# Value products of the cache attention one step later, row maximum behind the second key transpose

## The reference, cut to what matters

```python
def _online_update(carry, sc, ck):
    m, l, acc = carry
    m_new = jnp.maximum(m, sc.max(-1))
    corr = jnp.exp(m - m_new)
    p = jnp.exp(sc - m_new[..., None])
    acc = acc * corr[..., None] + jnp.einsum('bhtk,bkr->bhtr', p, ck.astype(jnp.float32))
    return (m_new, l * corr + p.sum(-1), acc)

def page_step(carry, pages):
    ck = cache_ckv[layer, pages]
    kp = cache_kpe[layer, pages]
    return _online_update(carry, _latent_scores(q_lat, q_pe, ck, kp), ck), None
```

## Time and profile before

| what | value |
|---|---|
| median of 3 runs | 972.66 us |
| lowest and highest | 965.53 and 984.15 us |
| the profiled execution | 984.15 us |
| its span on the core | 982.1 us |
| mean granted TensorE clock in it | 0.932 |
| PE busy | 880.4 us (90%) |
| DVE busy | 448.3 us (46%) |
| ACT and POOL busy | 266.9 and 120.0 us |

### The profile page before, as it was taken

How to read it: one execution, slowest core, us unless ns; L and a number is a source line. 1 busy time by engine, 2 the same in 40 slices (tenths; PEclk the granted TensorE clock), 3 DMA queues, 4 the chain that set the end, 5 groups by cost and what they waited for, 6 DMA issues and landing times.

```text
span 982.1 us, 20045 instructions
## 1 busy us (share of the span) xinstructions
PE 880.4 (90%) x8856; PEld 795.1 (81%) x8856; DVE 448.3 (46%) x614; ACT 266.9 (27%) x420; POOL 120.0 (12%) x151
## 2 busy tenths in 40 slices
PE   3999887888787999477799979999999999999996
PEld 2998876777676776355568969999999999999996
DVE  5355475675723343599803355343333344222222
ACT  5333211211122333421214343222222322222222
POOL 7002134334200000454000000000000000000000
PEclk9999899999987999579758989999999999999999
DMA  9423558677611000500122221222332222322202
GB/s 277 149 70 99 199 217 306 225 267 280 249 45 43 1 1 1 154 1 0 44 93 86 87 86 43 85 85 87 107 105 85 85 85 85 107 87 75 87 30 87
DMA packets 71571, 105.78 MB, mean 108 GB/s; under 512 B 7500, under 2 KB 63220, under 8 KB 67284
## 3 DMA queue, kind: packets, MB, share of 16 engines
q1 hardware_dynamic: 63940, 62.74, 20.2%
q0 software_dynamic: 7568, 42.11, 11.7%
HBM read 100.85 MB, written 4.00 MB: 107 GB/s over the span
## 4 chain that ended last, share of the span: by engine, by line
PE 78%; DVE 11%; issue 4%; ACT 2%; DMA 2%; POOL 1%; SPq 0%; DVEq 0%; POOLq 0%; ACTq 0%
PE pair L707 9%; PE pair L709 9%; PE pair L708 9%; PE pair L692 7%; PE pair L694 7%; PE pair L693 7%; PE pair L877 4%; PE pair L901 3%; DVE QD L1910 2%; PE pair L993 2%; PE pair L971 2%; PE pair L970 2%; PE pair L725 2%; DVE KT L1684 1%; PE pair L726 1%
## 5 line engine op out<-in xcount | busy, mean ns | idle before, releaser
L707 PE MATMUL pair<-xhi,whi 128*128 128x260 f32 x736 | 209.7, 285 | 4.6 <-DVE xlo L1591 4.6
L708 PE MATMUL pair<-xlo,whi 128*128 128x260 f32 x736 | 208.8, 284 | 0.0
L709 PE MATMUL pair<-xhi,wlo 128*128 128x260 f32 x736 | 208.6, 283 | 0.0
L707 PEld LDWEIGHTS pair<-xhi,whi 128*128 128x128 f32 x736 | 139.8, 190 | 5.0 <-issue 5.0
L708 PEld LDWEIGHTS pair<-xlo,whi 128*128 128x128 f32 x736 | 140.0, 190 | 0.0
L709 PEld LDWEIGHTS pair<-xhi,wlo 128*128 128x128 f32 x736 | 139.7, 190 | 0.0
L694 PE MATMUL pair<-hhi,wlo 128*128 128x260 f32 x352 | 99.4, 282 | 0.0
L692 PE MATMUL pair<-hhi,whi 128*128 128x260 f32 x352 | 99.3, 282 | 0.0
L693 PE MATMUL pair<-hlo,whi 128*128 128x260 f32 x352 | 99.2, 282 | 0.0
L1684 DVE STREAM_TRANSPOSE KT<-KC 128x2048 uint32<-128x2048 uint32 x32 | 73.7, 2304 | 2.6 <-DMA KP<-in_cache_kpe,icur 2.5
L692 PEld LDWEIGHTS pair<-hhi,whi 128*128 128x128 f32 x352 | 66.3, 188 | 0.0
(11 more groups left out here) (329 smaller groups left out, 1781.7 us busy)
## 6 DMA issues: line engine op xcount, KB each, us to landing
wraw<-in_w_gate SPq DMA_DIRECT2D x11, 1024.0 KB, 5.4
wraw<-in_w_up SPq DMA_DIRECT2D x11, 1024.0 KB, 5.4
wraw<-in_w_down SPq DMA_DIRECT2D x8, 1024.0 KB, 5.0
X<-in_x_prompt SPq DMA_DIRECT2D x8, 512.0 KB, 5.4
wraw<-in_w_in SPq DMA_DIRECT2D x4, 1024.0 KB, 5.9
wsame<-in_w_in SPq DMA_DIRECT2D x4, 1024.0 KB, 6.0
wraw<-in_w_out SPq DMA_DIRECT2D x4, 1024.0 KB, 6.6
wraw<-in_w_down SPq DMA_DIRECT2D x4, 768.0 KB, 4.3
```

The source lines that it names most:

```text
L707: mm(out, h[:, k, c], xhi[:, k, tok], start=k == 0, stop=False)
L708: mm(out, h[:, k, c], xlo[:, k, tok], start=False, stop=False)
L709: ins = mm(out, l[:, k, c], xhi[:, k, tok], start=False, stop=k == KD - 1)
```

## The change

In PE's stream the value products of step n-1 stand behind the second half of the scores of step n, where those of step n stood behind its spread. The fourth dense piece of an odd step now stands ahead of the spread. The products of the last step stand behind two `keys_up`. In DVE's stream `cache_probs(n - 1)` comes between the two transposes, and `cache_max(n)` behind the second. ACT's stream follows through `before_spread`. GpSimd's and SP's streams are as they were.

```diff
 def before_spread(n):
 
-    return 16 + 3 * n + n // 2 + 3 if n < STEPS else PIECES
+    return 16 + 4 * n + 4 - (n + 2) // 2 if n < STEPS else PIECES
...
                 dense_piece(k)
                 dense_piece(k + 1)
                 cache_scores(n, 1)
-                dense_piece(k + 2)
+                if n:
+                    cache_values(n - 1)
+                for k in range(k + 2, before_spread(n)):
+                    dense_piece(k)
                 cache_spread(n)
-                k += 3
-                if n % 2 == 1:
-                    dense_piece(k)
-                    k += 1
-                cache_values(n)
+                k = before_spread(n)
             assert k == PIECES
...
             keys_up(0)
             keys_up(1)
+            cache_values(STEPS - 1)
             keys_up(2)
             keys_up(3)
...
                 if n == 11:
                     hi(10)
-            evacuate(dense_done(PIECES - 1))
             hi(11)
...
                 cache_keys(2 * n + 1)
-                cache_max(n)
+                if n:
+                    cache_probs(n - 1)
                 if n + 1 < STEPS:
                     cache_keys(2 * n + 2)
-                cache_probs(n)
+                cache_max(n)
...
+            cache_probs(STEPS - 1)
             lo(11)
```

## The result

The changed kernel takes 1048.72 us (median of 4, 1042.84 to 1054.87); the kernel before, beside it, takes 976.89. The ratio is 1.0823, with a 95% interval of 1.0697 to 1.0949. The forecast was 1038 us, with a range of 1010 to 1062. The profiled executions are 984.15 and 1049.89 us, 66 us apart.

The account below looks back on a forecast made before the run. PE, busy nine tenths, bounded the kernel; the move closes a loop over the five-buffer ring, 13.97 us a step. That ends the stage 45 us later; with 20 for the clock, 65 on 972.66 gives 1038 us, range 1010 to 1062.

Parts of the forecast that it names:

- The ring: Five buffers for cache rows: the gather of half 2n+5 waits for step n's value products, closing a loop of 13.97 us.
- The size of the loop: Cache stage, each step: products, GpSimd, KP landing, transposes and scores sum to 13.97 us, plus 1.43 for the low clock.
- Rival C: Loop in the cache stage: clock low throughout, scores and products both slow, 2.83 us longer, 1058 us; chance 15 in 100.
- Rival B: Loop in the cache stage: it is closed but the clock stays at 2.4 GHz, 1018 us; chance 24 in 100.
- The end of the stage: Cache stage: last dense piece ends 45 us later by the loops, with 20 for the clock 65 us together.
- The even half has slack: Cache stage: the even half's transpose, maximum, exponential and spread have 5 us of slack before the scores that need them.
- The steps on ACT cost nothing: ACT in the cache stage: later exponential and cache_out waits are over before the maximum; without the loop 0.4 us each.
- DVE's wait: DVE's transpose of each odd half from 5 on waits for KP's DMA, 14 times some 5 us.
- (1): DVE: probabilities of step n-1 ahead of half 2n+2's transpose, maximum behind; with (2) at most 10.0 down to 8.4 a step.
- (2): PE: value products of step n-1 behind step n's second scores; both gaps of PE, 1.2 to 1.8 us a step, would close.
- rival A: Cache stage: gaps close, the ring doesn't bind, PE bounds at 8.4 us a step; 29 us saved, 944 us; 3 in 100.
- The sum against the median: Whole kernel: 65 us on the profiled 984.15 would give 1049; against the median of 972.66 the forecast is 1038 us.

Follow-up runs that it names:

- e9: The changed kernel with six ring buffers in place of five and v not kept, run a second time: 979.38 us, 0.998 of the kernel before.
- e1: The kernel before with four ring buffers in place of five, all orders as before: 1028.03 us, 1.059 of the kernel before.
- e10: The changed kernel with index copies and KP gathers of a pair of halves ahead of GpSimd's wait for the value products: 1014.51 us, 1.044 of before.
- e8: The changed kernel with DVE's order of before, so PE's and ACT's new order alone, run a second time: 1044.62 us, 1.075 of the kernel before.
- e5: The kernel before with DVE's new order alone, PE's and ACT's order and the ring of five as before: 1054.23 us, 1.028 of the kernel before.
- r1: The changed kernel itself run again, nothing altered: 1048.69 us, 1.076 of the kernel before by medians.
- e7: The changed kernel with 18 matmuls into unused columns ahead of the second scores of steps 2 to 15: 1022.03 us, 1.049 of the kernel before.
- e11: The kernel before with dense pieces moved behind both halves of the scores, and KP gathered ahead of the products' wait: 965.42 us, 0.994 of before.

## Why the prediction was right, point by point

**The ring is the path that becomes the bound: shown.** More buffers remove the loss (e9), fewer make it in the old order (e1), a shorter path through the gather makes it smaller (e10), and PE's order alone makes the whole of it (e8). The new order on DVE isn't needed for the loss (e8), and PE's new order costs nothing once there are buffers enough (e9). The DMA engines are filled less than before (0.48 from 150 to 300 us, for 0.72 in rows 2), so it isn't transfer time in general. That DVE's order alone would cost nothing isn't shown: e5 was slower, by a loop of its own.

**The size of the loop.** The 14 odd transposes start at 135.02 to 335.06: 13 turns of 15.39 us. The forecast was 13.97 and 1.43, 15.40. That agreement is in part luck: errors of up to 0.5 us cancel, and two more traces with the same loop, r1 and e8, have turns of 15.74 and 15.76. By terms, means over the 13 turns (with 0.16 for the handovers they make the 15.39):

| term | predicted | measured |
|---|---|---|
| products | 1.93, and 1.43 for the clock | 2.88 |
| GpSimd's start to DVE's transpose | 7.59 | 7.34 |
| transposes | 2.90 | 2.90 |
| scores, first matmul to the products | 1.40 | 2.11 |

I put the clock's price on the products alone. In fact the scores ran at half clock in most turns, being the first in the loop after the gap (2.09 us in the turn above), and the products often came back part of the way (2.11 to 3.64). Against e7, which has 1.91 and 1.14 at full clock, the clock costs 1.94 a turn in place of 1.43: 0.97 on each. Three things hid the 0.51. The scores at full clock are 1.14 in the loop and not 1.40: the products start 1.14 behind the first score matmul, and the 1.40 were read up to DVE's start. The products at full clock are 1.91. And GpSimd's path was 0.25 shorter, since KP's landing came to 5.4 on average for the 5.8 that I took. The prediction had named that as a way to be wrong, but it doesn't hold from trace to trace: in r1 and e8 that path is 7.6 us, as predicted. The 3.36 us that I took for products at half clock were not the whole of it either: the slowest took 3.64. Rival C had both pieces at half clock in every turn. For the scores that is nearly what came, for the products it isn't. Rival B, which had the clock at full, needed the filler of e7 to come true.

The Trainium skill's page "TensorE: Matmul & The Clock Gate", section "HAM oscillation", tells of tiles that each start at the lower clock behind a wait for a DMA. The trace agrees, with the 2.09 us of the scores for 1.14. The Trainium skill's page "DMA: Bandwidth & Descriptors", section "Anatomy of one DMA", has a fit that, taken over KC and KP together, gives an estimate of 5.0 us. From the issue of KC at 207.67 to the landing of KP at 214.05 there are 6.4, so the measurement decides against the estimate here.

**The end of the stage.** The last dense piece ended at 345.32, predicted 344.8; before it was 279.84, so 65.5 us against the sum of 65. In r1 the maxima are 4.6 us further apart, so agreement to half a us is luck as well.

**The even half has slack: right.** DVE waited a little for 8 of them, but PE had only one wait a step for keys, at the odd half. (By the prediction's own terms DVE is through with the odd half at 10.6 us, not 10.8; nothing hangs on it.) **The steps on ACT cost nothing: right**, with one thing wrong beside it: I wrote that PE's wait for spread would be gone. It is still there in 12 steps, up to 1.14 us (8.8 in all, 10.2 in 16 before), since the exponential follows a maximum that came later. It lies outside the loop.

**DVE's wait mis-sized.** I wrote "14 times some 5 us". That is PE's gap, 2.4 to 6.3 us, 4.6 on average. DVE had done all it could before, and waited 6.3 to 10.2. The steps, too, are spread wider than the 14 to 16 us that I wrote, from 13 to 18.

**The gain of (1) and (2): almost nothing, even free of the ring.** e9 gives 0.998, where rival A priced the closed gaps at 29 us for 14 steps. In e9 the maxima are 4.1 us closer than before, no more than two traces of one kernel differ. With six buffers DVE still waits for KP in 18 places: the changed order asks for the even transpose ahead of the maximum, so a late gather now holds up the exponential as well. That reading is argued from the waits; no run separates it.

**The sum against the median.** The forecast is 11 us low against 1048.72, and none of that is the stage: the shift of 65 from profile to profile came out as 66. I made the sum against an execution of 984.15 us and then took 11.5 off for the median. One thing that differs between such executions is told in the last section, at its first point: 16 us in one far stage, which the two profiled executions happened to share. How many of the untraced executions of either kernel had them isn't shown, so the 11 us stay open.

## What to carry to other kernels

A ring's buffer is freed by its last reader, so moving that reader one step later costs a step of prefetch, though no transfer is touched. Before such a move, add up the path from that reader through issue, landing and the next consumer back to it, and compare it with the step; if it is longer, the buffers must grow with the move, or what needn't wait (here KP) be taken out of the wait. If a closed loop has a gap in it, and the trace shows a low clock behind such gaps, price the first work after the gap at that clock, and judge experiments on one stage by a row of that stage, since the total has noise from elsewhere.

## What the runs showed of the hardware

**A stage far behind the change has two levels.** The time behind the last maximum is 689 to 693 us in six of the fourteen traces of the table and 705 to 710 in the other eight, with nothing between. The same 32 matmuls tell them apart in every trace. Here in after, then in e8, each with a window:

```profile
L1127 PE MATMUL pair<-qe,Sst x32: 418/498/579, 552.9 to 580.6; 64*128 64x128 f32 x32
...
550.00:580.00 30.00, 28.31 (x97) 19.79 (x96) 1.82 (x6) 2.94 (x6) 0.00 (x0) 0.50 0.27 96
```

```profile
L1127 PE MATMUL pair<-qe,Sst x32: 272/322/373, 563.4 to 579.8; 64*128 64x128 f32 x32
...
563.00:580.00 17.00, 15.87 (x90) 11.37 (x88) 1.82 (x6) 2.56 (x5) 0.00 (x0) 1.00 0.37 134
```

Their median is 498 ns in one and 322 in the other. Shortly ahead of these matmuls the granted clock was at 0.50 in both. In e8 it was back at 1.00 as they began; in after it stayed at 0.50 throughout, though PE was busy for 28.31 of 30 us. Both profiled executions of the comparison, before and after, have the 498. The 16 us are of the size of the spread of before (965.53 to 984.15), of which I had put some 4 down to a stall at 167 us; its other executions weren't traced. What decides it was not tried.

**PE can stop with no wait that the trace shows.** In one group all four traces had 43 to 53 such stops on PE ahead of the small matmuls of the scores, 20 to 25 us in all, and the unchanged kernel took 55 us more. Later, on the same chip, e8 had one of 1.3 us, e9 six with 9.3 and e11 six with 8.0. A comparison across the groups would have shown an effect of 5% where there was none. What makes them isn't shown.

**Idle matmuls can pay.** 18 matmuls without use in a gap raised the granted clock from 0.82 to 0.98 and took 22 us off the stage (e7 against r1).
